# Routing inside the output projection of a hybrid decoder layer, with slots in rank order and weights loaded in earlier stages

## What is computed

```python
merged = sigmoid(gate_a) * (attn @ w_branch_attn) + sigmoid(gate_r) * (ret @ w_branch_ret)
x = x + merged @ w_out
xn = rms_norm(x, norm_ffn)
p_group = softmax(xn @ w_router_group + b_router_group)
g_idx, g_w = argmax(p_group), max(p_group)
fine = (xn @ w_router_expert + b_router_expert)[the 8 of group g_idx]
top_p, top_i = top_k(softmax(fine), 2)
gates = g_w * top_p / sum(top_p)
experts = g_idx * 8 + top_i
y = sum over the two: gates * ((silu(xn @ w_gate[e]) * (xn @ w_up[e])) @ w_down[e])
x = x + y
```

## Time and profile before

| what | value |
|---|---|
| median of three runs | 2093.12 us (2091.94 to 2093.45) |
| the profiled execution, its own time | 2094.2 us |
| span in its trace, first to last instruction | 2092.6 us |
| busy: TensorE (PE), its weight loads (PEld) | 1853.2 us, 1575.1 us |
| busy: VectorE (DVE), ScalarE (ACT), GpSimd (POOL) | 1138.7 us, 852.8 us, 353.6 us |
| moved by DMA | 333 MB, 159 GB/s over the span |

### The profile page before, as it was taken

How to read it: one execution, slowest core, us unless ns; L and a number is a source line. 1 busy time by engine, 2 the same in 40 slices (tenths; PEclk the granted TensorE clock), 3 DMA queues, 4 the chain that set the end, 5 groups by cost and what they waited for, 6 DMA issues and landing times. The chain is left out here.

```text
span 2092.6 us, 28719 instructions
## 1 busy us (share of the span) xinstructions
PE 1853.2 (89%) x9822; PEld 1575.1 (75%) x9822; DVE 1138.7 (54%) x1736; ACT 852.8 (41%) x1496; POOL 353.6 (17%) x446
## 2 busy tenths in 40 slices
PE   7989997999997999999998969915999999999960
PEld 5867775999997888887877958704888888888840
DVE  4266656211102333334345443363999999999947
ACT  4255556111111212122212121113777777777734
POOL 2023322000000212122120100022311111111104
PEclk9999999999998999999997989957999999999985
DMA  6121102222213002020203443253999999999946
GB/s 186 49 67 24 48 21 61 72 82 70 81 51 119 21 23 71 13 80 23 81 3 123 149 119 121 78 206 114 395 378 381 377 376 379 375 379 379 374 171 246
DMA packets 185473, 333.00 MB, mean 159 GB/s; under 512 B 36016, under 2 KB 117456, under 8 KB 184320
## 3 DMA queue, kind: packets, MB, share of 16 engines
q1 hardware_dynamic: 163872, 277.57, 37.7%
q0 software_dynamic: 20720, 53.21, 7.1%
q10 hardware_dynamic: 816, 1.38, 0.4%
HBM read 304.08 MB, written 46.33 MB: 167 GB/s over the span
## 5 line engine op out<-in xcount | busy, mean ns | idle before, releaser
L2090 DVE TENSOR_TENSOR e_Lg<-e_rawg,e_Hg 128x1024 fp32r<-128x1024 f32 x128 | 148.4, 1219 | 12.0 <-ACT e_Hg L2043 12.0
L2090 DVE TENSOR_TENSOR e_Ld<-e_rawd,e_Hd 128x1024 fp32r<-128x1024 f32 x124 | 143.3, 1218 | 0.0
L2090 DVE TENSOR_TENSOR e_Lu<-e_rawu,e_Hu 128x1024 fp32r<-128x1024 f32 x124 | 143.2, 1214 | 0.0
L2043 ACT ACTIVATE e_Hg<-e_rawg 128x1024 fp32r<-128x1024 f32 x128 | 124.8, 1049 | 5.2 <-PE bank L152 5.2
L150 PE MATMUL bank<-r_wH,xH 128*128 128x512 f32 (+1 forms) x288 | 121.3, 421 | 6.3 <-DVE r_wL L1270 3.6
L2043 ACT ACTIVATE e_Hu<-e_rawu 128x1024 fp32r<-128x1024 f32 x124 | 121.0, 1060 | 0.0
L2043 ACT ACTIVATE e_Hd<-e_rawd 128x1024 fp32r<-128x1024 f32 x124 | 120.7, 1050 | 0.0
L152 PE MATMUL bank<-r_wH,xL 128*128 128x512 f32 (+1 forms) x288 | 116.2, 403 | 0.0
L151 PE MATMUL bank<-r_wL,xH 128*128 128x512 f32 (+1 forms) x288 | 115.6, 402 | 0.0
L1032 DVE TENSOR_TENSOR b_wL<-raw,b_wH 128x1024 fp32r<-128x1024 f32 x24 | 29.2, 1221 | 148.3 <-ACT b_wH L1005 148.3
L150 PE MATMUL bank<-e_Hg,e_xH 128*128 128x512 f32 x256 | 101.8, 398 | 3.1 <-DVE e_xL L2096 3.1
(11 more groups left out here) (388 smaller groups left out, 4682.2 us busy)
## 6 DMA issues: line engine op xcount, KB each, us to landing
e_rawg<-in_w_gate SPq DMA_DIRECT2D x128, 512.0 KB, 6.1
e_rawu<-in_w_up SPq DMA_DIRECT2D x128, 512.0 KB
e_rawd<-in_w_down SPq DMA_DIRECT2D x124, 512.0 KB, 6.8
raw<-in_w_in SPq DMA_DIRECT2D x51, 512.0 KB, 3.9
c_Y<-y_d SPq DMA_DIRECT2D x8, 1024.0 KB, 13.4
gate_t<-b_gr_s POOLq DMA_DIRECT2D x8, 528.0 KB, 2.9
m_t<-b_m_s POOLq DMA_DIRECT2D x8, 528.0 KB, 3.6
m_gate<-gate_t POOLq DMA_DIRECT2D x8, 528.0 KB, 4.0
```

The source lines that it names most:

```text
L2043: act.activation(H[kind][:, q], raw[kind][:, q], ACT.Copy).then_inc(w_hi[kind], 1)
L2090: dve.tensor_tensor(L[kind][:, q], raw[kind][:, q], H[kind][:, q].bitcast(F32), ALU.subtract).then_inc(w_lo[kind], 1)
```

## The change

- The five later pieces of `w_out` are loaded in the merge, into room at the top of SBUF (`ch.more`).
- There is no routing stage. Each tile's routing is done inside the output projection: `choose` (group, two experts, one-hot rows, a running count `cum`), `count` (TensorE: rank of each token within its expert, from this tile's earlier rows and the sum of earlier tiles), `place` (slot number), `fill` (POOL: two scatters), `exponentials` and `weights` (gates).
- A token of rank r at expert e has the slot r * 32 + e, so the slot is known without the counts of later tiles. An expert's list is then read from `toktab` with a stride of 32 entries.
- The router's product has 40 columns instead of 36 (four padding columns after the group columns).
- TensorE's order is project half 0, turn of the tile before, project half 1, route of the tile before, count of the one before that.
- Expert 0's weights are loaded when the last projection is done, into the room of the activations; their gate halves and the up high halves are made in this stage. The up low halves and the loads of expert 1's gate and up weights are in the expert stage.
- The overflow's table is computed behind the last tile; its scatters are made in the expert stage, by POOL, two for each of experts 2 to 10.
- Expert 0's slot list and rows are fetched at the end of the output projection, and the lists of experts 1 and 2.

```diff
@@ stage_merge, SP
                         sp.dma_start(raw[:, s], ch.w_ret[:, :, ds(m * P, P)]).then_inc(w_in[s], 16)
+                for q in range(3, KT):
+                    sp.dma_start(ch.more[:, q - 3], ch.w_out[:, :, q * P:(q + 1) * P]).then_inc(ch.w_sems["out"][q], 16)
                 sp.wait_ge(lo_done, KT)
                 first_loads(sp, ch, "out")
@@ stage_out, SP
-                for q in range(3, KT):
-                    sp.dma_start(raw(q), ch.w_out[:, :, q * P:(q + 1) * P]).then_inc(w_in[q], 16)
                 for t in range(NT):
...
+                    if t == 1:
+                        sp.wait_ge(lo_done, KT)
+                        for dst, src in ((iota, ch.c["iota"][:, 0:NE]), (groups, ch.c["groups"]), (before, ch.c["before"]), (ones, ch.c["ones"])):
+                            sp.dma_start(dst[:], src).then_inc(table_in, 16)
+                        sp.dma_start(ch.tokens[:], ch.c["tokens"]).then_inc(table_in, 16)
+                sp.wait_ge(mm_done, NT)
+                for kind in "gud":
+                    for q in range(NQ):
+                        expert_chunk(sp, ch, kind, 0, q)
@@ stage_out, POOL
+                def fill(t):
+                    m = rows_of(t)
+                    if t == 0:
+                        pool.wait_ge(table_in, 16 * 5)
+                    pool.wait_ge(placed, t + 1)
+                    for k in range(2):
+                        pool.indirect_dma_start(out=ch.toktab, out_offset=bass.IndirectOffsetOnAxis(ap=slots[0:m, t, k:k + 1], axis=0),
+                                                in_=ch.tokens[0:m, t, k], in_offset=None, bounds_check=NE * P - 1, oob_is_err=False).then_inc(scat, 16)
+
+                for t in range(NT):
+                    store(t)
+                    if t >= 2:
+                        fill(t - 2)
+                fill(NT - 2)
                 for s in range(2):
...
+                fill(NT - 1)
+                pool.wait_ge(ch.e_go, 1)
+                pool.wait_ge(scat, 16 * 2 * NT)
+                expert_slots(pool, ch, 0)
+                expert_gather(pool, ch, 0)
+                expert_slots(pool, ch, 1)
+                expert_slots(pool, ch, 2)
@@ stage_out, ScalarE
-                for t in range(NT + 1):
-                    if t < NT:
-                        front(t)
-                    if t >= 1:
-                        back(t - 1)
+                def exponentials(t):
+                    m = rows_of(t)
+                    act.wait_ge(keyed, t + 1)
+                    act.activation(eg[0:m], lg[0:m, 0:NG], ACT.Exp, bias=less[0:m, 0:1], accum_out=den[0:m, 0:1]).then_inc(e_done, 1)
+                    act.activation(den[0:m, 1:2], fm8[0:m, 1:2], ACT.Exp, bias=less[0:m, 1:2]).then_inc(e_done, 1)
...
+                front(0)
+                for t in range(1, NT):
+                    back(t - 1)
+                    front(t)
+                    exponentials(t - 1)
+                split_hi("g", (0, 1))
+                back(NT - 1)
+                split_hi("g", (2, 3))
+                exponentials(NT - 1)
+                split_hi("u", range(NQ))
@@ stage_out, VectorE
+                def choose(t):
...
+                    done(dve.max(gm8[0:m], lg[0:m, 0:EPG]))
+                    done(dve.max_index(gi8[0:m], gm8[0:m], lg[0:m, 0:EPG]))
+                    done(dve.tensor_copy(gidx[0:m], gi8[0:m, 0:1]))
+                    done(dve.tensor_scalar(fine[0:m], groups[0:m], gidx[0:m], NEG, ALU.not_equal, ALU.mult))
+                    done(dve.tensor_tensor(fine[0:m], fine[0:m], lg[0:m, EPG:], ALU.add))
+                    done(dve.max(fm8[0:m], fine[0:m]))
+                    done(dve.max_index(fi8[0:m], fm8[0:m], fine[0:m]))
...
+                def place(t):
+                    m = rows_of(t)
+                    dve.wait_ge(rank_mm, t + 1)
+                    dve.tensor_tensor(slotp[0:m], hot[0:m, t], banks[7][0:m, None, 0:NE].broadcast_to([m, 2, NE]), ALU.mult).then_inc(ranked, 1)
+                    dve.wait_ge(ranked, t + 1)
+                    done(dve.tensor_reduce(rank[0:m, t], slotp[0:m], AX, ALU.add))
+                    done(dve.scalar_tensor_tensor(out=slotf[0:m], in0=rank[0:m, t], scalar=float(NE), in1=eid[0:m, t], op0=ALU.mult, op1=ALU.add))
+                    dve.tensor_copy(slots[0:m, t], slotf[0:m]).then_inc(placed, 1)
...
+                front(0)
+                for t in range(1, NT):
+                    back(t - 1)
+                    front(t)
+                    choose(t - 1)
                     if t >= 2:
+                        place(t - 2)
+                    weights(t - 1)
+                back(NT - 1)
+                place(NT - 2)
+                split_lo("g", 0)
+                split_lo("g", 1)
+                choose(NT - 1)
+                place(NT - 1)
+                split_lo("g", 2)
+                split_lo("g", 3)
+                weights(NT - 1)
+                overflow()
@@ stage_out, TensorE
+                def count(t):
+                    m, s = rows_of(t), t % 2
+                    pe.wait_ge(chosen, t + 1)
+                    pe.wait_ge(ranked, t)
+                    mm = pe.matmul(banks[7][0:m, 0:NE], before[0:m, 0:m], both[0:m, s], start=True, stop=(t == 0))
+                    if t:
+                        mm = pe.matmul(banks[7][0:m, 0:NE], ones[:, 0:m], cum[:, t], start=False, stop=True)
+                    mm.then_inc(rank_mm, 1)
+
+                for t in range(NT):
+                    project(t, 0)
+                    if t >= 1:
+                        turn(t - 1)
+                    project(t, 1)
+                    if t >= 1:
+                        route(t - 1)
                     if t >= 2:
...
+                        count(t - 2)
+                turn(NT - 1)
+                count(NT - 2)
+                route(NT - 1)
+                count(NT - 1)
@@ expert lists
+def expert_slots(pool, ch, e):
...
+    pool.dma_start(ch.e_idx[:, e % IDX], ch.toktab[0:NE * P, :].rearrange("(r e) o -> r e o", e=NE)[:, e, :]).then_inc(ch.e_idx_in[e % IDX], 16)
@@ stage_experts
+                load("g", 1)
+                load("u", 1)
                 walk(sp, body)
...
                     if e >= 1:
                         scatter(e - 1)
+                    if 2 <= e < 2 + NT:
+                        fill_beyond(e - 2)
...
                 rows_lo(0)
+                split_lo("u", 0)
                 walk(dve, body)
```

More of the change, by code:

```diff
@@ L1595, in stage_out @@
     sem = ch.sem
[L1596 removed]
+    w_in, hi_done, lo_done, mm_done, x_in = ch.w_sems["out"], sem("o_hi"), sem("o_lo"), sem("o_mm"), [sem("o_x0"), sem("o_x1")]
     tab_in, add_done, sq_done, ms_done, root_done, rstd_done, xn_done = (
         sem("o_tab"), sem("o_add"), sem("o_sq"), sem("o_ms"), sem("o_root"), sem("o_rstd"), sem("o_xn"))
[L1599 to L1600 removed]
+    x2_st, xn_st, turned, t_out0, t_out1, r_mm = ([sem("o_x2s0"), sem("o_x2s1")], [sem("o_xns0"), sem("o_xns1")], sem("o_t"), sem("o_to0"), sem("o_to1"),
+                                                  sem("o_rmm"))
+    pad_done, step, lg_done, keyed, chosen, rank_mm, ranked, placed, e_done, total_mm = (
+        sem("o_pad"), sem("t_step"), sem("t_lg"), sem("t_keyed"), sem("t_chosen"), sem("t_rmm"), sem("t_ranked"), sem("t_placed"), sem("t_exp"), sem("t_tmm"))
+    table_in, empty, scat = sem("t_tab"), sem("t_empty"), sem("t_scat")
     NH = D // 512
+    NL = 2 * EPG + NG * EPG - EPG
     with ExitStack() as st:
         sb = ch.sbuf(st)
[L1604 to L1605 removed]
+        raw = lambda q: ch.raw[:, q] if q < 3 else ch.more[:, q - 3]
         wH, wL = sb("o_wH", [P, KT, D], F32R), sb("o_wL", [P, KT, D], F32R)
@@ L1672, in _, with done @@
                     dve.tensor_tensor(wL[:, :, cols], raw(q), wH[:, :, cols].bitcast(F32), ALU.subtract).then_inc(lo_done, 1)
+                dve.wait_ge(lo_done, KT)
+                dve.memset(hot[:], 0.0).then_inc(pad_done, 1)
+                dve.memset(rank[:], 0.0).then_inc(pad_done, 1)
                 dve.wait_ge(tab_in, 16 * 5)
+                dve.wait_ge(pad_done, 4)
+                count = [0]
+                def done(ins):
+                    ins.then_inc(step, 1)
+                    count[0] += 1
+                    dve.wait_ge(step, count[0])
                 def front(t):
@@ new lines, in weights @@
+                def weights(t):
+                    m = rows_of(t)
+                    dve.wait_ge(e_done, 2 * t + 2)
+                    done(dve.reciprocal(den[0:m, 2:3], den[0:m, 0:1]))
+                    done(dve.tensor_scalar(den[0:m, 3:4], den[0:m, 1:2], 1.0, None, ALU.add))
+                    done(dve.reciprocal(den[0:m, 3:4], den[0:m, 3:4]))
+                    done(dve.tensor_tensor(ch.gates[0:m, t, 0:1], den[0:m, 2:3], den[0:m, 3:4], ALU.mult))
+                    done(dve.tensor_tensor(ch.gates[0:m, t, 1:2], ch.gates[0:m, t, 0:1], den[0:m, 1:2], ALU.mult))
@@ L1960, in stage_experts @@
         y = sb("e_y", [P, D])
```

(3 more changed lines are left out.)

365 lines of the change are left out of this document (145 added, 220 removed).

## The result

Before 2093.28 us (median of 4 runs, 2091.94 to 2094.41), after 2034.47 us (4 runs, 2030.74 to 2035.44): ratio 0.9712, 95% interval [0.9698, 0.9726], 58.8 us less. The forecast was 2043.3 us in a range from 2037: the sign was right, the gain was underestimated by 9 us, and the result lies outside the range.

What follows compares the result with a forecast made beforehand. TensorE was taken to bound the output projection and experts, with 85 us of thin work between. Expert 0's first gate product moves from 1437.06 to 1387.2 (1351.1 + 36.1), 49.9 us less: 2043.3 us, range 2037 to 2051, to 2055 with rival 1.

Steps and rivals of the forecast that it cites:

- if the experts then run as before: Expert stage: TensorE busy 500.00 of 500 us, so only an earlier first gate product (1437.06 to 1387.2) counts, 49.9 us.
- Head, -6.0: Start of the output projection: weights loaded earlier remove the late start and the 3.14 us stall; 6.0 us, bounds 3.1 and 7.
- X0': End of tile 0's projection in the changed kernel, forecast at 1240.4 against 1246.4 before.
- Loop: Output projection's tiles with routing inside: about 14.2 us a tile against 13.75, a count 0.45, TensorE not waiting.
- X8': End of tile 8's projection in the changed kernel, forecast at 1351.1, 0.9 us earlier than before.
- Rival 1: Tile loop: the 1.1 us margin is used up and TensorE waits before each turn; 2055 us, chance 0.10.
- Table loads: ScalarE in the tile loop: two reloads a tile, 1.28 us each; the one before Sqrt lengthens the chain by 1.05.
- rival 5: ScalarE: each table switch costs another 1.28 us around its load, 0.2 a tile and 1.3 in the tail; 2046, chance 0.05.
- Tail, 36.1: From the end of tile 8's projection to expert 0's first gate product: 36.1 us, against 85.1 before.
- rival 6: Tail: descriptors are not held up by VectorE, so the last two scatters take 1.9 us instead of 3.6; 2041.6, chance 0.05.
- Rivals 2, 3 and 4: Gather waits for all 18 scatters, 2065 (0.04); expert transfers become bound, 2107 (0.02); overlap given back, within 0.2% of before (0.02).
- the sign given for rival 2: Tail: POOL issuing more than four scatters behind X8' would show that the scatters don't spread.

Runs made afterwards that it cites:

- b_rel0: The kernel before with e_idxs' 64 bytes moved behind e_y, so the expert products' two operands begin at the same place modulo 256 bytes: 2082.32 us.
- a_rel64: The changed kernel with 64 unused bytes per partition ahead of e_xH, putting the expert products' operands 64 bytes apart: 2047.87 us.
- u_wout: The changed kernel with the five later pieces of the output weights loaded at the start of the output projection again: 2040.57 us.
- v_all: The changed kernel with xH, xL rows of 1088 columns, 32 bytes ahead of kv_wH, two slot lists and one low half moved into the expert stage: 2024.82 us.
- a_rel32: The changed kernel with a pad of 32 bytes ahead of e_xH, putting the expert products' operands 32 bytes apart: 2049.02 us.
- s64_r64: The changed kernel with the expert weights moved up by 64 bytes and a 64-byte pad ahead of e_xH (operands 64 bytes apart): 2047.34 us.
- a_rel128: The changed kernel with a pad of 128 bytes ahead of e_xH, putting the expert products' operands 128 bytes apart: 2044.06 us.
- t_slots: The changed kernel with the slot lists of experts 1 and 2 fetched at the head of the expert stage: 2035.75 us.
- t_no_over: The changed kernel without its table of the rows beyond 128 of an expert, two memsets in its place: 2033.96 us.

## Why the prediction was wrong

**The step that failed** is the premise of the whole price, "if the experts then run as before", with its reason, that inside the expert stage "nothing can be won by moving other work". A busy share of 500.00 in 500 us says that TensorE never waits. It does not say that a matmul takes its shortest time: 0.2333 us against 0.2271. The change moved no work there, but two small tiles, and with them `e_xH`. The difference of 0.4 us an expert is 11.9 us from the first gate product to the end; b_rel0 and a_rel64 show 11.0 and 13.4 in the medians, and 12.5 and 12.7 in the stretch behind the first gate product. Without the 11.9 the changed kernel would stand at 2046.4, inside the range and 3 us above the forecast. The diff shows it only in where two allocations went, and I had not worked out addresses. The range had no case for this.

**Head, -6.0:** right. Start 1227.1 on before's scale as forecast, no stall, X0' = 1241.1 (forecast 1240.4); u_wout gives 6.1.

**Loop:** right. 14.25 us a tile for 14.2, a count 0.45 as taken, margin 1.03 for 1.1, and X8' = 1352.2 on before's scale for 1351.1. Rival 1 (waits at the turns) didn't come, though 1 us was all there was.

**Table loads:** right, and rival 5 is out. Between the end of the squaring (its accumulator is read until 1322.25) and the load lie 0.02 us, between the load and the root 0.01, and between the root's end and the next load 0.03. The Trainium skill (ScalarE: Activation LUTs, What ACT_TABLE_LOAD costs) adds a drain of 1.38 us to each; the trace disagrees here as it did before.

**Tail, 36.1:** measured 37.5, with two errors that partly cancel. Up to the gather's issue it took 26.6 where 28.3 was forecast: the end of the last two scatters was met (22.3 for 22.4), but their landing and the slot list came 1.7 us sooner, since the 3.04 us taken from the earlier trace rows held a stage change that is no longer there. The step "then the stage change, and TensorE's transposes are wanted at 32.7" failed the other way. VectorE ended at +29.8, near the 30.8 forecast, and I left 1.9 us for the change of stage. It took 3.7 behind VectorE and 4.6 behind GpSimd, so the transposes came at +34.1 and the rows, for which TensorE had waited before, were waiting for it. The two slot lists behind the gather, which I had not put on the path, seem to have been on it by 0.3 us.

**Scatters and rival 6:** the last two took 2.11 and 0.88 (forecast: 3.6 with the gap; measured 3.29). The Trainium skill (SBUF — State Buffer, Who interferes with whom) holds that tensor_tensor doesn't hold up descriptor generation, for a reason that it marks as inferred. Measured, the first took 2.11 us while VectorE subtracted for 2.3 us beside it, and 0.97 in v_all where the subtraction ended 0.2 us after its start. Within the changed kernel the scatter at 1360.27, beside the subtractions from 1359.97, took 1.80 us and the next one, begun when they had ended, 0.97; those in the loop took 1.00 to 1.05. So the issue of a scatter is longer beside the subtractions, and going by the row was right. What holds it up is open: the same section of the Trainium skill also says that a VectorE instruction with two inputs in SBUF, as these have, contends with a GpSimd instruction that reads SBUF, and no run here tells such a read from descriptor generation.

**Rivals 2, 3 and 4** cost nothing, but the sign given for rival 2, more than four scatters behind X8', did come: there are six. The prediction's own tail places tiles 6, 7 and 8 behind that mark, which makes six, so the sign was set wrong; POOL was not behind, as the end of the last two was met. TensorE is busy for 500.00 of 500 us in the experts. Its one wait before that, 1.66 us ahead of expert 1's gate product for the low half of the token rows, stands in both kernels alike, so the weights of expert 1 came in time.

In all, up to the first gate product 49.9 us were forecast and 47.4 came; 11.9 came behind it from a place that the prediction had declared untouched.

## What to carry to other kernels

When a change adds, drops or moves an allocation, work out the addresses of every operand behind it, and compare the mean spacing of the same matmuls, not only the busy share: a TensorE that is busy all the time can still be 2.7% off its pace. Let both operands of an fp32r product begin at the same place modulo 256 bytes, with row lengths a multiple of 64 numbers; in this kernel the pads cost 32 bytes to 2 KB a partition. And count the end of a block as a step of its own, from the last instruction of each engine that issues DMAs or computes, not from the last one on the chain.

## What the runs showed of the hardware that I had not expected

- 24 matmuls of 128x512 (fp32r, at full clock) take 5.45 us with the two operands at the same place modulo 256 bytes and 5.56 to 5.60 at 32, 64 or 128 bytes apart, whatever the absolute place (0 or 64 above a multiple of 128) and however busy the DMAs are (share 1.00 in the experts, 0.29 in the projection, where half of the slices lay 128 bytes off: 5.54 against 5.65). Why was not found out. At half clock there is no difference: 0.427 us a matmul in both kernels.
- The transfers follow the pace oddly. At distance 0 the gate pieces take 10.3 to 12.2 us to land and the scatters of an expert's results 4.24 to 4.35 us to issue; at 32 and 64 they take 6.0 to 6.3 and 1.47 to 1.48 (a_rel32, a_rel64, s64_r64 and the kernel before); at 128 6.1 and 3.38. It costs nothing, as TensorE never waits; the DMA share is 1.00 in both kernels, at 379 and 386 GB/s. That a stage 2.2% faster in its use fills the queues is a reading that no run tested, and a_rel128, slow in pace but with long scatters, doesn't fit it. From the page of the changed kernel, the costliest groups (busy us, mean ns) and then the issues (count, KB each, median us to landing; the earlier trace rows had 6.1):

```profile
L2062 POOL DMA_INDIRECT y_d<-e_y,e_idxs x32 | 135.6, 4239 | 202.0 <-DVE e_y L2161 200.4
...
e_rawg<-in_w_gate SPq DMA_DIRECT2D x128, 512.0 KB, 12.2
```

- A change of block cost 3.4 to 3.5 us behind VectorE's last instruction or 4.6 us behind GpSimd's last issue of a DMA, in two kernels each: t_slots and v_all, the changed kernel and t_no_over.
